# Second block of a two-block transformer: projecting the rows before their norm, and the order at the start

## What is computed

```python
def rmsnorm(x, g):
    y = x * lax.rsqrt(jnp.mean(x * x, axis=-1, keepdims=True) + RMS_EPS)
    return y * g

def hybrid_layer(x, norm_g, w_in, ...):          # twice; x = rms_norm(x, g_final) of the first block
    h = rmsnorm(x, norm_g)
    proj = h @ w_in                              # 8388 columns: heads, gates, merge gates
    ...                                          # three attentions, gated, merged
    return x + merged @ w_out
```

## Time and profile before

| what | us |
|---|---|
| median of three runs | 1653.62 (1651.47 to 1655.75) |
| the profiled execution, device time | 1652.93 |
| its span, first to last instruction | 1651.0 |
| busy in the span: TensorE, VectorE, ScalarE, GpSimd | 1544.5, 940.7, 674.7, 322.3 |
| DMA | 234.20 MB, 142 GB/s in the mean |

### The profile page before, as it was taken

One profiled execution on the slowest core, in us unless ns is written; L12 is line 12 of the kernel. 1 busy time (PEld: TensorE's weight loads), 2 busy tenths in 40 slices (PEclk: granted clock), 3 DMA queues, 4 the chain that ended last, 5 costly groups with the idle time before them and its releaser, 6 DMA issues.

```text
span 1651.0 us, 23520 instructions
## 1 busy us (share of the span) xinstructions
PE 1544.5 (94%) x9299; PEld 1267.7 (77%) x9299; DVE 940.7 (57%) x1318; ACT 674.7 (41%) x1045; POOL 322.3 (20%) x265
## 2 busy tenths in 40 slices
PE   5899989999999999799989999799999989999997
PEld 3675457888888887665679998688988877898886
DVE  2745536445444456635466667678634656874456
ACT  4335444321122214435453334544554544445554
POOL 1216511100000001416110000221145111203431
PEclk9999999999999999899989999899999989999999
DMA  8426842223322332328645554545423445463342
GB/s 313 159 70 240 290 115 77 84 95 102 102 87 91 102 103 77 103 92 289 162 132 192 180 178 153 160 166 179 154 85 125 149 129 171 137 196 103 104 141 89
DMA packets 168974, 234.20 MB, mean 142 GB/s; under 512 B 8968, under 2 KB 116520, under 8 KB 168752
## 3 DMA queue, kind: packets, MB, share of 16 engines
q1 hardware_dynamic: 168880, 232.89, 43.2%
HBM read 231.82 MB, written 1.05 MB: 141 GB/s over the span
## 4 chain that ended last, share of the span: by engine, by line
PE 79%; DVE 11%; ACT 4%; issue 2%; POOL 2%; DMA 2%; SPq 0%; POOLq 0%; DVEq 0%; ACTq 0%
PE psum L691 22%; PE psum L692 21%; PE psum L693 21%; DVE wl L1540 3%; PE psum L915 3%; PE psum L948 3%; PE psum L706 2%; PE psum L935 2%; ACT wh L1213 2%; DVE work L1643 1%; PE psum L920 1%; DVE roped L1746 1%; DVE hTl L1622 1%; POOL work L2180 1%; DVE smax L1780 1%
## 5 line engine op out<-in xcount | busy, mean ns | idle before, releaser
L1540 DVE TENSOR_TENSOR wl<-raw,wh 128x2048 fp32r<-128x2048 f32 (+1 forms) x170 | 387.4, 2279 | 259.7 <-ACT wh L1430 150.3
L691 PE MATMUL psum<-hTh,wh 128*128 128x256 f32 (+1 forms) x1376 | 430.6, 313 | 14.2 <-DVE hTl L1622 7.6
L692 PE MATMUL psum<-hTl,wh 128*128 128x256 f32 (+1 forms) x1376 | 424.9, 309 | 0.0
L693 PE MATMUL psum<-hTh,wl 128*128 128x256 f32 (+1 forms) x1376 | 424.8, 309 | 0.0
L691 PEld LDWEIGHTS psum<-hTh,wh 128*128 128x128 f32 x1376 | 264.1, 192 | 32.6 <-issue 8.5
L692 PEld LDWEIGHTS psum<-hTl,wh 128*128 128x128 f32 x1376 | 264.4, 192 | 12.9
L693 PEld LDWEIGHTS psum<-hTh,wl 128*128 128x128 f32 x1376 | 264.2, 192 | 12.5
L1430 ACT ACTIVATE wh<-raw 128x2048 fp32r<-128x2048 f32 x62 | 118.9, 1917 | 364.4 <-PE psum L693 364.4
L1213 ACT ACTIVATE wh<-raw 128x2048 fp32r<-128x2048 f32 (+2 forms) x108 | 202.5, 1875 | 139.1 <-PE psum L693 126.4
L691 PE MATMUL psum<-wh,hTh 128*128 128x512 f32 (+3 forms) x576 | 227.2, 394 | 28.9 <-DVE hTl L1622 15.7
L2180 POOL TENSOR_SCALAR work<-work,share 128x256 f32<-128x256 f32 (+4 forms) x118 | 165.8, 1416 | 306.1 <-DVE share L1796 306.0
(11 more groups left out here) (165 smaller groups left out, 1811.0 us busy)
## 6 DMA issues: line engine op xcount, KB each, us to landing
raw<-in_w_in SPq DMA_DIRECT2D x54, 1024.0 KB, 4.9
raw<-in_w_ada SPq DMA_DIRECT2D x48, 1024.0 KB, 5.5
raw<-in_w_gate SPq DMA_DIRECT2D x22, 1024.0 KB, 5.0
raw<-in_w_up SPq DMA_DIRECT2D x22, 1024.0 KB, 5.0
raw<-in_w_down SPq DMA_DIRECT2D x22, 1024.0 KB, 4.7
raw<-in_w_in SPq DMA_DIRECT2D x16, 768.0 KB, 4.3
raw<-in_w_out SPq DMA_DIRECT2D x8, 1024.0 KB, 4.8
raw<-in_w_out SPq DMA_DIRECT2D x16, 384.0 KB, 7.3
```

The lines of the kernel that those rows point to most:

```text
L691: pe.matmul(o, left[0], right[0], start=first, stop=False)
L692: pe.matmul(o, left[0], right[1], start=False, stop=False)
L693: return pe.matmul(o, left[1], right[0], start=False, stop=last)
L1540: dve.tensor_tensor(wl[:, w % SPLIT, 0:m], raw[:, u % RING, 0:m], wh[:, w % SPLIT, 0:m].bitcast(F32), ALU.subtract).then_inc(lo_ready, 1)
```

## The change

- **The second block's norms.** TensorE turns `resid` itself (`turn_sums`), and the leading and low parts are made with a gain for each column: `norm_g_2` of layer 1, and the product of `g_final` and `norm_g_2` of layer 0 (`gain`, made at the start; a sixth list loads `g_final`). They go to columns 256 to 511 of `hTh` and `hTl`, from where the nine blocks read. The low part is one fused instruction a chunk (`low_pairs`) instead of a product into `work` and half a subtraction. ScalarE's evictions of the nine blocks take the root of the row as scale (`root`).
- **The roots.** Layer 1: as before, but the scaling is gone from the path. Layer 0: GpSimd multiplies the residual by `g_final` into `xn2`, four products of 128x512 (`both_roots`), ScalarE squares both `resid` and `xn2`, and GpSimd makes the root of the first norm (`first_root`) and the root of both together, (eps * e + q) to the power -1/2 with e the mean square and eps of `resid` and q the mean square of `xn2`. VectorE then writes the first block's result over `resid` (four fused products in place).
- **The normalised rows** for the gates are made later: ScalarE scales them at the end of block 1 (four instructions), TensorE turns them between the halves of blocks 2 (three pairs) and 3 (one pair), and both engines evict them as they come (`turn_normed`, `lead_normed`, `low_normed`).
- **The start.** Tile 0 is turned before the wait for the lists; the second sums come before the first spread; the third sums come in front of group 0 and the spread of it in front of group 1; the context rows are issued behind unit 6. VectorE keeps the first sums after taking the second, and takes the third between the two pairs of tile rows.

The core of the diff, indentation cut by eight:

```diff
+AGAIN, AGAIN_BANKS = {2: (0, 1, 2), 3: (3,)}, (7, 3, 4, 7)
+def gain(l, k):
+    at = 56 + k if l else 64 + k
+    return cols[:, at:at + 1]
...
-           ("norm1", 1), ("proj1", 1), ("att1", 1), ("wout1", 1), ("norm1b", 1), ("ffn", 1),
-           ("final", 0)]
+           ("norm1", 1), ("proj1", 1), ("att1", 1), ("wout1", 1), ("norm1b", 1), ("ffn", 1)]
...
+    load(grows[48:56, :], a["g_final"].rearrange("(k p) -> k p", p=P), lists_loaded)
-        if u == FIRST_UNITS[0]:
+        if u == FIRST_UNITS[0] + 2:
...
+    def turn_sums(l):
+        row0[0], xn0[0] = c.now(hT_ready), c.now(xn_ready)
+        c.next(hT_ready, 8)
+        c.next(xn_ready, 4)
+        for n in range(2):
+            if l == 0:
+                pe.wait_ge(resid_ready, 8 + 2 * (n + 1))
+            else:
+                pe.wait_ge(evac_dve, c.now(evac_dve) - 1 + n)
+            for kk, b in enumerate(norm_banks("norm2", l, 0)):
+                o = bank(b) if n == 0 else ps[b]
+                for x in range(2):
+                    k = 2 * kk + x
+                    mm = pe.transpose(o[:, SEQ * x + P * n:SEQ * x + P * n + P],
+                                      resid[:, n, P * k:P * k + P], ident[:, :])
+                if n == 1:
+                    mm.then_inc(xnT_done, 1)
+                    freed[b] = (hT_ready, row0[0] + kk + 1)
+    def turn_normed(pairs):
+        pe.wait_ge(xn_ready, xn0[0] + 4)
+        for kk in pairs:
+            b = AGAIN_BANKS[kk]
+            o = bank(b)
+            for x in range(4):
+                k, n = 2 * kk + x // 2, x % 2
+                mm = pe.transpose(o[:, P * x:P * x + P], xn2[:, n, P * k:P * k + P], ident[:, :])
+            mm.then_inc(xnT_done, 1)
+            freed[b] = (hT_ready, row0[0] + 4 + kk + 1)
-        made = ada_sums(*ADA_HEAD[0], 0)
+        made = [ada_sums(*ADA_HEAD[0], 0)]
+        turn_rows("norm1", 0, 0, tiles=(0,))
-        pe.transpose(ps[4][:, 0:48], grows[:, :], ident[0:48, 0:48])
+        pe.transpose(ps[4][:, 0:56], grows[:, :], ident[0:56, 0:56])
-        turn_rows("norm1", 0, 0, tiles=(0,))
-        ada_spread(*made)
-        made = ada_sums(*ADA_HEAD[1], 1)
-        ada_spread(*made)
+        made.append(ada_sums(*ADA_HEAD[1], 1))
+        ada_spread(*made[0], 0)
+        ada_spread(*made[1])
...
-            spread()
-        return {(0, 1): lambda: sums(2), (0, 2): in_front_of_context, (0, 3): spread,
+        return {(0, 0): lambda: sums(2), (0, 1): spread, (0, 2): in_front_of_context, (0, 3): spread,
...
+            if blocks is SECOND_BLOCKS and b in AGAIN:
+                turn_normed(AGAIN[b])
+        at = SEQ if blocks is SECOND_BLOCKS else 0
-                 [(lambda n, t=t: (hTh[:, n, P * t:P * t + P], hTl[:, n, P * t:P * t + P]), lo, hi)
+                 [(lambda n, at=at + P * t: (hTh[:, n, at:at + P], hTl[:, n, at:at + P]), lo, hi)
...
-        if step in ("norm1", "norm1b", "norm2") and (step, l) != ("norm1", 0):
-            norm({"norm1": 2, "norm1b": len(tiles_of(l)) // 2, "norm2": 1}[step], step, l)
+        if step in ("norm1", "norm1b") and (step, l) != ("norm1", 0):
+            norm({"norm1": 2, "norm1b": len(tiles_of(l)) // 2}[step], step, l)
-        if step == "final":
-            c.next(xn_ready, 4)
+        if step == "norm2":
+            turn_sums(l)
...
+            pe.wait_ge(hT_ready, row0[0] + 8)
...
+            if not first and b in AGAIN:
+                lead_normed(l, AGAIN[b])
+                if not first and b == 0:
+                    act.wait_ge(rstd_ready, c.next(rstd_ready))
...
-                    evac_group(rs[:, nq % 2, lo:hi], (0, hi - lo), ring=ring)
+                    evac_group(rs[:, nq % 2, lo:hi], (0, hi - lo), ring=ring, scale=root(t))
-                    evac_group(v, (0, hi - lo), ring=ring)
+                    evac_group(v, (0, hi - lo), ring=ring, scale=root(t))
+            if not first and b == 1:
+                for t in X:
+                    for hf in range(2):
+                        half = slice(512 * hf, 512 * hf + 512)
+                        act.activation(xn2[:, t, half], (resid if l else xn2)[:, t, half], ACT.Copy,
+                                       scale=root(t)).then_inc(xn_ready, 1)
...
-                if which < 2:
-                    act.wait_ge(mod_ready, 2 * l + which + 2)
+                act.wait_ge(mod_ready, 2 * l + which + 2)
+    turned0 = [0]
+    def lead_pairs(pairs, banks, at, scale):
+        for kk in pairs:
+            act.wait_ge(xnT_done, turned0[0] + kk + 1)
+            for x in range(2):
+                k = 2 * kk + x
+                act.activation(hTh[:, k, at:at + SEQ], ps[banks[kk]][:, SEQ * x:SEQ * x + SEQ], ACT.Copy,
+                               scale=scale(k)).then_inc(hTh_ready, 1)
+    def lead_normed(l, pairs):
+        lead_pairs(pairs, AGAIN_BANKS, 0, lambda k: cols[:, 48 + 8 * l + k:49 + 8 * l + k])
+    def norm2(l):
+        def squares(src, t, hf, at):
+            half = slice(512 * hf, 512 * hf + 512)
+            act.activation(scr[:, at, half], src[:, t, half], ACT.Square, scale=D ** -0.5,
+                           accum_out=ss[:, at, hf:hf + 1]).then_inc(row_squares, 1)
+        def sums(t, hf):
+            act.wait_ge(*rows_from[t][hf])
+            squares(resid, t, hf, t)
+        turned0[0] = c.now(xnT_done)
+        c.next(xnT_done, 8)
+        banks = norm_banks("norm2", l, 0)
+        split_ahead(1)
+        for t, hf in ((0, 0), (1, 0), (0, 1)) if l else ((0, 0), (0, 1)):
+            sums(t, hf)
+        if l == 0:
+            split_ahead()
+        lead_pairs((0, 1), banks, SEQ, lambda k: gain(l, k))
+        split_ahead()
+        lead_pairs((2, 3), banks, SEQ, lambda k: gain(l, k))
+        turned0[0] += 4
+        if l:
+            sums(1, 1)
+            return
+        for t in X:
+            for hf in range(2):
+                if t:
+                    sums(t, hf)
+                act.wait_ge(gained, c.next(gained))
+                squares(xn2, t, hf, 2 + t)
...
-        own(dve.tensor_copy(cols[:, 16:64], ps[4][:, 0:48]), cols_ready)
-        ada_keep(*ADA_HEAD[0])
+        link(dve.tensor_copy(cols[:, 16:72], ps[4][:, 0:56]))
+        own(dve.tensor_tensor(cols[:, 64:72], cols[:, 64:72], cols[:, 48:56], ALU.mult), cols_ready)
+        ada_keep(*ADA_HEAD[0], 0)
...
-            rows(0, (0, 1))
+            rows(0, (0,))
+            rows(0, (1,))
...
+    def low_pairs(pairs, banks, at, scale):
+        for kk in pairs:
+            dve.wait_ge(hTh_ready, c.next(hTh_ready, 2))
+            for x in range(2):
+                k = 2 * kk + x
+                ins = dve.scalar_tensor_tensor(
+                    out=hTl[:, k, at:at + SEQ], in0=ps[banks[kk]][:, SEQ * x:SEQ * x + SEQ], scalar=scale(k),
+                    in1=hTh[:, k, at:at + SEQ].bitcast(F32), op0=ALU.mult, op1=ALU.subtract)
+            own(ins, hT_ready)
+    def low_normed(l, pairs):
+        low_pairs(pairs, AGAIN_BANKS, 0, lambda k: cols[:, 48 + 8 * l + k:49 + 8 * l + k])
+    def norm2(l):
+        banks = norm_banks("norm2", l, 0)
+        split_ahead(1)
+        low_pairs((0, 1), banks, SEQ, lambda k: gain(l, k))
+        split_ahead()
+        low_pairs((2, 3), banks, SEQ, lambda k: gain(l, k))
+        c.next(xn_ready, 4)
+        if l:
+            return
+        for t in X:
+            dve.wait_ge(first_root, t + 1)
+            for hf in range(2):
+                r = resid[:, t, 512 * hf:512 * hf + 512]
+                link(dve.scalar_tensor_tensor(out=r, in0=r, scalar=rstd[:, t:t + 1],
+                                              in1=grow[:, 0, 512 * hf:512 * hf + 512], op0=ALU.mult,
+                                              op1=ALU.mult))
...
+            if t == 0 and not first and b in AGAIN:
+                low_normed(l, AGAIN[b])
...
-            norm(1, 2, l, step)
-            c.next(xn_ready, 4)
+            if l == 0:
+                dve.wait_ge(gains_loaded, 32)
+            norm2(l)
...
+    def both_roots():
+        def chain(ins):
+            ins.then_inc(pool_chain, 1)
+            pool.wait_ge(pool_chain, c.next(pool_chain))
+        pool.wait_ge(gains_loaded, 32)
+        for t in X:
+            for hf in range(2):
+                half = slice(512 * hf, 512 * hf + 512)
+                pool.wait_ge(resid_ready, 8 + 2 * t + hf + 1)
+                pool.tensor_tensor(xn2[:, t, half], resid[:, t, half], grow[:, 0, half], ALU.mult)\
+                    .then_inc(gained, 1)
+        for t in X:
+            e, q = ss[:, t, 0:1], ss[:, 2 + t, 0:1]
+            pool.wait_ge(row_squares, c.next(row_squares, 2 + t))
+            chain(pool.tensor_scalar(e, e, ss[:, t, 1:2], EPS, ALU.add, ALU.add))
+            pool.tensor_tensor(rstd[:, t:t + 1], e, mhalf[:, 0:1], ALU.pow).then_inc(first_root, 1)
+            pool.wait_ge(row_squares, c.next(row_squares, 2 - t))
+            chain(pool.tensor_scalar(e, e, EPS, q, ALU.mult, ALU.add))
```

(2 more changed lines are left out.)

60 lines of the change are left out of this document (28 added, 32 removed).

## The result

The changed kernel takes 1641.86 us in the median of 7 runs (1641.13 to 1652.18), against 1654.92 us for the kernel before in the same comparison (7 runs, 1651.47 to 1656.22): a ratio of 0.9938, interval 0.9922 to 0.9955. The forecast was 1641.5 us, with a range of 1634 to 1648.5. The gain is 13.1 us by the medians and 10.3 us by the ratio (7.4 to 12.9 by its interval).

What follows compares the result with a forecast made beforehand. TensorE, busy 94% of the span, was taken to bound the kernel, so only its idle stretches could win; layer 0's 5.3, layer 1's 3.4 and the start's 3.5 us made 12.2 us, forecast 1641.5 us (1634 to 1648.5).

Steps and rivals of the forecast that it cites:

- The three places: TensorE stands still between the two blocks, in front of layer 1's projection and in the first 52.1 us; only there can time be won.
- Part 1: Layer 0, between the blocks: roots leave the path; first projection product 8.0 us earlier, after 1.8 us lost to GpSimd's collision.
- Up to the middle of block 1: Layer 0's projection: VectorE sets the pace, unit 2's low part ends at 1049.6 instead of 1056.8, gain 7.2 us.
- Part 2: Blocks 2 and 3: 16 more transposes per layer cost TensorE 1.9 us; evictions and low parts cost nothing, or up to 3 us.
- Layer 0: Layer 0's net gain: 7.2 us from the roots less 1.9 us for the transposes, 5.3 us.
- Layer 1: First product 3.8 us earlier, clock loss 1.2 instead of 2.7 us, less 1.9 for transposes: 3.4 us gained.
- The start: First 52.1 us: second conditioning product 2.0 us earlier, third moved off the path (1.9 us); 3.5 us gained, between 0 and 6.
- (a): Projection takes the gain back: late low parts from a full VectorE stop TensorE, 3 us per layer; 1647.5 us, chance 0.14.
- (d): Transposes ahead are held until the old time by a bank or semaphore, 1.9 us more per layer; 1654 us, chance 0.04.
- (b): The start gives nothing because context and units share DMA; 1645 us, or 1648 if context rows come later; chance 0.12.
- (c): Gain above forecast: clock stays up in both pauses, no collision (1.8 us), start 2 us better; 1636.5 us, chance 0.12.
- (e): Slower: GpSimd's four products of p us each delay the last residual row by 3 x (p - 1.3); chance 0.03.

Runs made afterwards that it cites:

- later rows: Changed kernel with VectorE's four in-place products and the masks moved behind unit 2's low part, into block 1: 1644.72 us, ratio 0.994.
- small products: Changed kernel with GpSimd's four gain products cut from 512 to 64 columns (result not right): 1637.97 us, ratio 0.9899.
- doubled products: Changed kernel with each of GpSimd's four gain products made twice: 1648.45 us, ratio 0.9965.
- filler: Changed kernel with idle identity transposes on TensorE in the pauses (20 and 28 in layer 0, 20 in layer 1): 1647.7 us, ratio 0.996.
- mended filler: Changed kernel with 18 and 27 idle identity transposes in layer 0's pause, 18 in layer 1's into a free bank: 1639.78 us, ratio 0.992.
- the last two kernels: Changed kernel with mended filler, later rows and ten idle transposes in block 1: 1637.85 us; the same with GpSimd's products held until VectorE's first low part: 1638.41 us.

## Why the prediction was right

The places and the mechanisms were right, and the total came out: 1641.5 us forecast, 1641.86 measured. That it is so close is in part luck. The forecast's 12.2 us lie between the 10.3 us of the ratio and the 13.1 of the medians; in the two traces a start and a layer 0 below the forecast are made up by a layer 1 above it, and that surplus is a chance of the execution.

- **The three places.** The time was won at the three places where TensorE stood still, and TensorE's busy time did not change. Right.
- **Part 1, the first product** at 8.0 us earlier: 7.4 (1045.44 against 1037.12, less the 0.95 us that the trace was ahead by then). Of its terms the additions' wait was near, 1.4 for 1.8; the fused low parts are 0.44 us each for the 0.47 taken; what failed is "VectorE then has the low part of unit 0, 2.29 us": it stands behind the fourth product and takes 3.28. The Trainium skill (GPSIMD Engine Reference, Specifications) says that GpSimd contends with VectorE's instructions that have two SBUF inputs; the rows agree (0.69 us to 1.21, 2.29 to 3.28, and 0.44 for the low parts, which read PSUM). The sum's term counted three of the four collisions: 1.8 us where the four measured 2.4.
- **Up to the middle of block 1** at 7.2 us: 6.4, and 5.3 against the trace of the new start alone, whose clock was low in this pause for 10.2 us and not 13.7. "VectorE and no longer the norm sets the pace" was right for the first product and wrong for unit 2: the low part waited 1.23 us for ScalarE's leading half, which waited for TensorE's first half block at half clock. The later rows alone, which shorten VectorE's chain by over 4 us, moved nothing; with the clock kept up they were worth 1.6 us. The end of that low part, forecast at 1049.6 in times of before, stands at 1050.55 in those times, 0.95 us late; that the changed kernel's own trace reads 1049.60 is a coincidence.
- **Part 2** at 1.9 us a layer: 1.55 and 1.6 by the kernel without them. Right in kind (no cover for TensorE, full cover for the rest), some 20% too dear, since a run of transposes reaches beyond the start of the next product: the twelve last 1.47 us, and the product begins 1.23 us behind their start.
- **Layer 0** at 5.3: 4.9 in the two traces, 2.4 with the slower trace after and the faster one before.
- **Layer 1** at 3.4: 5.4 in the two traces, 2.7 to 3.7 against the four kernels with the same layer 1. The first product is 3.9 us earlier relative to the last row, forecast 3.8. The error is the clock: the forecast took 1.2 us of loss out of a range of 0 to 2.7 and looked only at the stretch in the earlier trace rows. Low time behind the first product fell from 5.5 to 3.1 us, worth 1.2, of which 1.0 is there at block 1's middle (1357.71 against 1369.16); and a second fall in the kernel before, at 1370.0 for 3.4 us, which the forecast had not looked for, is absent: 1.7 more. This last part is a chance of the execution: in the traces of the old start, the small products, the later rows and the doubled products, which make the same layer 1, and of the kernel without normalised rows, a fall of 3.4 us at this place, 20 us behind the pause, is there. 3.9 + 1.0 + 1.7 - 1.6 = 5.0; the rest, 0.4, I did not follow. Without the chance the term was right.
- **The start** at 3.5: 2.6 in the two traces, 2.3 to 3.0 by all runs. The second conditioning product's first half began at 16.53, as wanted, the spreads followed, and the context's rows did no harm. VectorE's low part was ready at 26.44, where the forecast put the first group at 26.6. What failed is that the third product costs nothing in front of it. Its units were issued at 17.66 us and behind it, and landed near 23.2 and 26.35: TensorE waited 1.70 and 2.11 us for them. "1 MB takes 3.3 us" prices one transfer at the mean rate of the start; between 16 and 30 us the DMA engines were full (a share of 0.99 to 1.05) and the units took 5.4 to 9.2 us from issue to landing. And with both units "there by 26" the second half of that product still has to run, which the forecast's own 26.6 leaves out: it took 1.94 us at a granted clock of 0.50, and the first group began at 28.22. So the move of the third product paid little: it takes 1.92 us away behind group 0 and puts 1.8 in front of it, and about 2 of the 2.6 us are the earlier second product's. Whether the context's megabyte, issued at 19.54, held up the second of these units was not tried.
- **Not in the forecast:** 1.7 us for a longer stretch at the lower clock around 838 us. No part of the change touches that stage. With the smaller start it stands against layer 1's surplus: 2.6 - 1.7 + 4.9 + 0.6 + 5.4 = 11.8.
- **The rivals.** (a) and (d) did not happen. (b) did not, but what it says of DMA is why the start gave less. (c) is refuted: the products do meet VectorE, and the clock fell in both new pauses, for 10.2 us in layer 0 and 3.4 in layer 1. (e) has a wrong formula: the additions do not lengthen with the product, the roots do; at twice the work the loss was 4.5 us by the ratios and 1.0 to 2.5 by the traces, where its formula, with p = 2.6 us, gives 3.9.

## What to carry to other kernels

Taking a norm off TensorE's path was worth nearly its whole chain here (a pause of 7.5 us for one of 14.9), but look at once for what the work now has in its way on the port between GpSimd and VectorE: count every instruction that has both inputs in SBUF, the one behind the last as well. Where a pause is shortened, the work behind it may still be set by the clock that the pause left behind; in layer 0 a filler helped only with the next waits shortened and filled too, while in layer 1 it was enough alone. And before a trace's totals are compared, subtract what the falls of the clock differ by: here single executions of one kernel lie up to 11 us apart, and distances between two instructions tell an edit of 1.5 us where the median doesn't, if more than one trace of each kind is at hand: two single traces were some 2 us apart in a stretch of the same code.

## What the runs showed of the hardware

- **VectorE and GpSimd take turns by instruction.** In these rows, with both engines waiting, one instruction of each goes in turn: VectorE's addition waits for the rest of GpSimd's product (0.69 to 1.21 us), never for two of them, and GpSimd's product of 1.27 us takes 3.32 when a low part of VectorE got in ahead. Even GpSimd's operation on one column (L2284), 0.30 us alone, took 2.22 us beside such a low part.
- **Granted clock.** With the filler in the pause the clock stayed at 1.00 over it and fell at the next waits in three kernels: for 6.8 us in two, with waits of some 1.7 and 1.3 us, and for 3.4 us in one, with waits of 0.67 and 1.25; where those were shortened and filled it did not fall, and where a wait of 1.88 us stood in front of the fill it fell again. Without the filler it fell in this pause in every kernel, for 3.4 us in the ones with small and with doubled products, for 13.7 in the kernel before and for 10.2 in the others. Four of these kernels (old start, small products, later rows, doubled products) had one more fall of 3.4 us in block 1, four (before, new start alone, changed, no normalised rows) had none; so a fall in block 1 needs no filler, and the filler alone does not prevent it. In layer 1, where the changed kernel's wait is 2.1 us, it stayed at 1.00 in the three kernels with the mended filler of 18 transposes, in one of them over waits of 0.67 and 1.26 us in block 1 too; so the length of a wait alone does not tell whether the clock falls.
- **It falls in other places too.** The stretch at the lower clock around 838 us was 10.2 or 13.7 us long in executions that are the same up to there but for the start. Which of the two an execution gets does not follow the edits: 10.2 before and in the last two kernels, 13.7 in the ten others. Its cause was not tried.
